# First norm of a three-block network: its weights come in as one row and are spread over the partitions by two products

## The reference, cut to what matters

```python
def _rmsnorm(x, g):
    xf = x.astype(jnp.float32)
    r = lax.rsqrt(jnp.mean(xf * xf, axis=-1, keepdims=True) + EPS)
    return (xf * r * g.astype(jnp.float32)).astype(x.dtype)
...
f = _swiglu(_rmsnorm(x, ffn1_pre_g[l]), ffn1_w_gate[l], ffn1_w_up[l], ffn1_w_down[l])
x = x + 0.5 * _rmsnorm(f, ffn1_post_g[l])
```

## Time and profile before

| | before |
|---|---|
| median of 3 runs | 2034.22 us (2034.13 to 2034.35) |
| profiled execution, its own time | 2034.27 us |
| its span | 2032.5 us |
| TensorE busy | 2015.1 us, 99% of the span |
| VectorE, GpSimd, ScalarE busy | 61%, 50%, 47% |
| granted TensorE clock, mean | 0.999 |
| DMA, mean over the span | 94 GB/s |
| DMA, 12.7 to 22.4 us | 295 GB/s |

### The profile page before, as it was taken

How to read it: one execution, slowest core, us unless ns; L and a number is a source line. 1 busy time by engine, 2 the same in 40 slices (tenths; PEclk the granted TensorE clock), 3 DMA queues, 4 the chain that set the end, 5 groups by cost and what they waited for, 6 DMA issues and landing times.

```text
span 2032.5 us, 30529 instructions
## 1 busy us (share of the span) xinstructions
PE 2015.1 (99%) x11856; PEld 1753.2 (86%) x11856; DVE 1234.5 (61%) x2038; ACT 951.5 (47%) x1777; POOL 1020.3 (50%) x576
## 2 busy tenths in 40 slices
PE   9999999999999999999999999999999999999998
PEld 8999988877788999988888878899888888888997
DVE  7877730877848777811356673965333676568553
ACT  5445623567754545623444544443433445353442
POOL 4666654346753766744434443465534443264542
PEclk9999999999999999999999999999999999999999
DMA  6333332311033333332322222333342222223332
GB/s 189 102 105 106 104 102 94 121 43 32 32 104 104 105 105 107 105 100 94 129 81 75 74 79 78 94 99 99 114 130 84 79 75 75 83 84 94 104 114 73
DMA packets 244287, 191.65 MB, mean 94 GB/s; under 512 B 6448, under 2 KB 208816, under 8 KB 243760
## 3 DMA queue, kind: packets, MB, share of 16 engines
q1 hardware_dynamic: 244144, 189.70, 30.6%
HBM read 187.58 MB, written 2.10 MB: 93 GB/s over the span
## 4 chain that ended last, share of the span: by engine, by line
PE 91%; DVE 5%; ACT 2%; issue 1%; SPq 0%; DMA 0%; POOL 0%; DVEq 0%; ACTq 0%
PE bank L2205 19%; PE bank L2206 19%; PE bank L2207 19%; PE bank L2338 9%; PE bank L2340 9%; PE bank L2339 9%; PE bank L2199 3%; PE bank L2496 1%; PE bank L2664 1%; PE bank L2516 1%; PE bank L2523 1%; DVE xs_part L1542 1%; DVE xs_lo L1567 1%; DVE xn L1441 0%; DVE x_tok L1446 0%
## 5 line engine op out<-in xcount | busy, mean ns | idle before, releaser
L708 POOL TENSOR_TENSOR w_lo<-w_raw,w_hi 128x1024 fp32r<-128x1024 f32 x216 | 536.8, 2495 | 470.2 <-ACT w_hi L864 469.8
L864 ACT ACTIVATE w_hi<-w_raw 128x1024 fp32r<-128x1024 f32 x271 | 283.2, 1053 | 197.2 <-DMA w_raw<-in_ffn_w_down 125.3
L2205 PE MATMUL bank<-xt_hi,w_hi 128*128 128x512 f32 (+1 forms) x640 | 243.4, 380 | 0.5
L2206 PE MATMUL bank<-xt_lo,w_hi 128*128 128x512 f32 (+1 forms) x640 | 239.3, 374 | 0.0
L2207 PE MATMUL bank<-xt_hi,w_lo 128*128 128x512 f32 (+1 forms) x640 | 239.3, 374 | 0.0
L2205 PE MATMUL bank<-w_hi,xt_hi 128*128 128x512 f32 (+1 forms) x456 | 178.2, 391 | 0.0
L2207 PE MATMUL bank<-w_hi,xt_lo 128*128 128x512 f32 (+1 forms) x456 | 174.4, 382 | 0.0
L2206 PE MATMUL bank<-w_lo,xt_hi 128*128 128x512 f32 (+1 forms) x456 | 174.3, 382 | 0.0
L2205 PEld LDWEIGHTS bank<-xt_hi,w_hi 128*128 128x128 f32 x640 | 120.5, 188 | 29.5 <-issue 6.7
L2207 PEld LDWEIGHTS bank<-xt_hi,w_lo 128*128 128x128 f32 x640 | 120.5, 188 | 22.0
L2206 PEld LDWEIGHTS bank<-xt_lo,w_hi 128*128 128x128 f32 x640 | 120.7, 189 | 19.6
(11 more groups left out here) (397 smaller groups left out, 5583.2 us busy)
## 6 DMA issues: line engine op xcount, KB each, us to landing
w_raw<-in_w_in SPq DMA_DIRECT2D x132, 512.0 KB, 3.8
w_raw<-in_ffn_w_down SPq DMA_DIRECT2D x44, 512.0 KB, 3.4
w_raw<-in_ffn_w_gate SPq DMA_DIRECT2D x43, 512.0 KB, 3.9
w_raw<-in_ffn_w_up SPq DMA_DIRECT2D x43, 512.0 KB, 3.8
w_raw<-in_w_out SPq DMA_DIRECT2D x24, 512.0 KB, 3.4
w_raw<-in_w_branch SPq DMA_DIRECT2D x24, 512.0 KB, 3.4
w_raw<-in_w_qkv SPq DMA_DIRECT2D x16, 512.0 KB, 3.8
x_tok<-in_x SPq DMA_DIRECT2D x4, 512.0 KB, 7.0
```

The lines of the kernel that those rows point to most:

```text
L708: pool.tensor_tensor(lo_slots[i], raw_slots[i], f32(hi_slots[i]), ALU.subtract).then_inc(lo_ready, 1)
L864: act.activation(hi_slots[i], raw_slots[i], ACT.Copy).then_inc(hi_ready, 1)
L2205: pe.matmul(out_ap, ah, bh, start=first, stop=False)
L2206: pe.matmul(out_ap, ah, bl, start=False, stop=False)
```

## The change

The row of weights is loaded as it is, 4 KB into partition 0 (`gain_row`), ahead of x chunk 0. GpSimd writes ones into a row of 128 (`one_row`). TensorE makes two products of that row of ones with the two halves of the weights' row, both operands fp32 and one partition deep, into banks 3 and 7, so that each partition there holds the weights. VectorE scales chunk 0 in two halves straight from these banks, then copies them into `g_pre`, which the later chunks read. The first half of chunk 0 now counts on `xn_first`, as that of chunk 1 did. The 36 fillers become 20 ahead of the two products and 10 behind them, and fillers write bank 6 instead of bank 7.

```diff
--- before.py
+++ after.py
@@ -183,6 +183,7 @@
             return t
 
         xn, junk = on("xn", [2, D], 88), on("junk", [D], 96, BF16)
+        gain_row, one_row = on("gain_row", [D], 98), on("one_row", [P], 0)
 
 
         def x_sum_tiles(name, home):
@@ -299,6 +300,8 @@
 
         bank = [ctx.enter_context(nc.psum_tensor(f"bank{i}", [P, SEQ], F32)) for i in range(8)]
 
+        gain_banks = (bank[3], bank[7])
+
         def f32(t):
 
             return t.bitcast(F32)
@@ -351,6 +354,7 @@
         w_used = sem("w_used")
         x_in = [sem(f"x_in{c}") for c in range(NC)]
         pre_in, post_in = sem("pre_in"), sem("post_in")
+        gain_spread = sem("gain_spread")
         tabs1_in, tabs2_in = sem("tabs1_in"), sem("tabs2_in")
         swap_in, swap_ready, count_in = sem("swap_in"), sem("swap_ready"), sem("count_in")
         decay_in = sem("decay_in")
@@ -584,8 +588,8 @@
             def load_x(c):
                 sp.dma_start(x_tok[:, c, :], x_v[:, c, :]).then_inc(x_in[c], 16)
 
+            sp.dma_start(gain_row[0:1, :], ffn1_pre_g).then_inc(pre_in, 16)
             load_x(0)
-            gain(g_pre, ffn1_pre_g, pre_in)
             load_x(1)
 
             def first_between(i):
@@ -695,8 +699,9 @@
 
         @block.gpsimd
         def _(pool):
+            pool.memset(one_row[0:1, :], 1.0).then_inc(pool_step, 1)
             pool.memset(ident[:, :], 0.0).then_inc(pool_step, 1)
-            pool.wait_ge(pool_step, 1)
+            pool.wait_ge(pool_step, 2)
             pool.affine_select(out=ident[:, :], in_=ident[:, :], compare_op=ALU.not_equal, fill=1.0, base=0,
                                pattern=[[-1, P]], channel_multiplier=1).then_inc(ident_ready, 1)
 
@@ -716,7 +721,7 @@
                 ins.then_inc(pool_step, 1)
                 pool.wait_ge(pool_step, steps[0])
 
-            steps[0] = 1
+            steps[0] = 2
 
             def out_low(pair):
 
@@ -1461,12 +1466,21 @@
 
                 dve.wait_ge(rtx_done, 4 * b + c + 1)
                 link(dve.reciprocal(inv_x[c % 2], root_x[c % 2]))
-                if c == 0:
+                if c == 0 and b > 0:
                     dve.wait_ge(pre_in, 16 * (b + 1))
                 if b in (0, 4) and c >= 2:
                     dve.wait_ge(tr_done, 2 * (4 * b + c - 1))
                 if b == 5 and c >= 2:
                     dve.wait_ge(out_done, 32)
+                if (b, c) == (0, 0):
+                    dve.wait_ge(gain_spread, 1)
+                    for half, done in enumerate((xn_first, xn_ready)):
+                        sl = cols(half, 512)
+                        dve.scalar_tensor_tensor(out=xn[:, 0, sl], in0=x_tok[:, 0, sl], scalar=inv_x[0],
+                                                 in1=gain_banks[half][:, :], op0=ALU.mult, op1=ALU.mult).then_inc(done, 1)
+                    dve.tensor_copy(g_pre[:, 0:512], gain_banks[0][:, :])
+                    link(dve.tensor_copy(g_pre[:, 512:D], gain_banks[1][:, :]))
+                    return
                 if b == 0 and c == 1:
                     dve.scalar_tensor_tensor(out=xn[:, 1, 0:512], in0=x_tok[:, 1, 0:512], scalar=inv_x[1],
                                              in1=g_pre[:, 0:512], op0=ALU.mult, op1=ALU.mult).then_inc(xn_first, 1)
@@ -2273,8 +2287,8 @@
             def turn_chunk(b, c):
 
                 for half, bk in enumerate((bank[c], bank[4 + c])):
-                    if half == 0 and (b, c) == (0, 1):
-                        pe.wait_ge(xn_first, 1)
+                    if half == 0 and b == 0 and c < 2:
+                        pe.wait_ge(xn_first, c + 1)
                     else:
                         pe.wait_ge(xn_ready, 4 * b + c + 1)
                     transposes(bk, [xn[:, c % 2, cols(4 * half + k)] for k in range(4)]).then_inc(tr_done, 1)
@@ -2421,10 +2435,15 @@
             def keep_busy(n):
 
                 for _ in range(n):
-                    pe.matmul(bank[7][:, 0:P], ident[:, :], ident[:, :], is_transpose=True)
+                    pe.matmul(bank[6][:, 0:P], ident[:, :], ident[:, :], is_transpose=True)
 
             pe.wait_ge(ident_ready, 1)
-            keep_busy(36)
+            keep_busy(20)
+            pe.wait_ge(pre_in, 16)
+            for half in range(2):
+                ins = pe.matmul(gain_banks[half][:, :], one_row[0:1, :], gain_row[0:1, cols(half, 512)], start=True, stop=True)
+            ins.then_inc(gain_spread, 1)
+            keep_busy(10)
             turn_chunk(0, 0)
             keep_busy(6)
             turn_chunk(0, 1)
```

## The result

| | before | changed |
|---|---|---|
| median of 22 runs | 2034.22 us | 2036.46 us |
| lowest, highest | 2034.05, 2034.56 | 2035.54, 2038.56 |
| profiled execution, its span | 2034.27, 2032.5 | 2038.41, 2036.6 |
| ratio to before, 95% interval | | 1.0013 (1.0007 to 1.0019) |

A forecast was written before the change was run, and what follows sets the result against it. TensorE, busy 2015.1 of 2032.5 us, was taken as the bound, so only its gapless start could move. VectorE's delay of +1.00 less 0.15 at chunk 3 gave +0.85, forecast 2035.1 us, range 2033.7 to 2036.9.

The forecast's parts named there:

- Points 1 and 2: Loads: row in front delays x chunk 0 by 0.44 us; 512 KB less brings chunk 1 1.1 to 1.9 earlier.
- point 6: VectorE: halves and two copies end at 10.52, so chunk 1 and the first feed-forward product come 1.00 us later.
- Point 3: GpSimd's memset of one row ahead of ident: 0.05 us, so fillers start at 1.58.
- Point 4, the price: The two fp32 products take four passes, 1.82 us at 2.4 GHz, plus 0.17 until the result: banks ready at 7.89.
- Point 4, the clock: Clock rise seen near 5.85 us, products starting at 5.90, so they were priced at 2.4 GHz, 1.82 us.
- second rival: The two products run at 1.2 GHz and cost 3.63 us: +2.66, 2036.9 us; chance 0.20.
- third rival: Clock stays low into the first feed-forward products: loss above 4.1 us, up to 8.5, 2042.8 us; chance 0.03.
- Point 5: Ten fillers behind the products: chunk 0's transposes start at 8.8 against 7.99, hidden because chunk 1 comes later.
- Point 7: Taken back at x chunk 3: TensorE's 0.15 us wait for its transposes goes, leaving TensorE 0.85 later.
- a sign of being wrong: Stated refutation: first feed-forward product before 12.65 us, or TensorE's gaps behind it growing.

The follow-up runs named there:

- e3: Changed kernel with 5 fillers ahead of the two products instead of 20: median 2034.96 us.
- e11: Changed kernel with 16 fillers ahead of the products instead of 20: 7 executions at 2035.08 to 2035.65 us, 4 at 2037.29 to 2037.65.
- e12: Changed kernel, GpSimd's first low part made to wait for VectorE's second half of x chunk 1: median 2035.80 us.
- e4: Changed kernel, chunk 1 also scaled from the banks, copies moved behind second slab's low part: 7 executions at 2035.22 to 2035.87 us, 4 at 2039.27 to 2039.60.
- e5: Kernel before, its 36 fillers replaced by 14 fp32 products of the identity, one partition deep: median 2034.83 us.
- e6: Kernel before, its 36 fillers replaced by 14 fp32 products of the identity, 128 partitions deep: median 2034.12 us.
- e2: Changed kernel with all 36 fillers ahead of the products, none behind: median 2039.16 us.
- e9: Changed kernel run again, nothing altered: 9 executions at 2035.76 to 2036.34 us, 2 at 2038.15 and 2038.40; gave its second trace, 2035.84.
- e1: Changed kernel with products 128 partitions deep, the row loaded behind x chunk 0: median 2035.84 us, traced execution 2034.84.
- e8: Kernel before with the first norm's weights left out, x in their place, and a 64-byte load into g_pre: median 2033.40 us.
- e10: Changed kernel, row loaded first into 32 partitions, products 128 deep, 12 fillers ahead and 8 behind, ScalarE copying: median 2033.97 us against 2034.28 before.

## Why the prediction was right or wrong

The forecast was 2035.1 in a range of 2033.7 to 2036.9; the median is 2036.46. The range holds it and the sign is right, but no execution of the changed kernel was as low as 2035.1, and the forecast's 0.85 is less than half of the 2.2 us. That the median lies inside is in part luck: 8 of 22 executions lie above the range, and the others owe some 0.7 us to a collision that no rival named.

*Points 1 and 2, the loads:* right, but for what they set free (point 6). x chunk 0 landed 0.3 to 0.5 later (4.62 and 4.75), chunk 1 at 7.06 in one trace and before 6.09 in the other (forecast 6.3 to 7.1), and VectorE had no use for it.

*Point 3:* the fillers started at 1.66, not 1.58: the extra memset costs 0.13.

*Point 4, the price:* right where the clock is up. Four records in 1.98 us against 1.82 and 0.17. The low level was priced at 3.63, with the 0.17 at 3.80, and measured 3.77 from first start to end. The Trainium skill, "FP8 and Floating Point Precision", section "TensorE Precision Notes", has four passes for true FP32; the traces agree: each product is two records, and records in mid-stream start 0.853 us apart at the low level, which is twice 512 columns at 1.2 GHz, and 0.43 at the high one.

*Point 4, the clock:* **this failed for a third of the executions.** The step took the rise at 5.85 as given, "since the clock rose right where they start". It varies from 4.8 to 6.2 over the traces, and the products, one partition deep, do not bring it: where it had not come when they began, it came 4.1 to 4.5 us after they had ended (e3, e11, e12, e4, the changed kernel), at 14.4 in the changed kernel's trace. The second rival had this, at 2036.9, but priced only the products. The trace adds ten fillers at 0.22 and eight transposes at the low level, which is the third rival's path short of its end: 2038.4, between the two. The argument against the second rival, that their operands feed the array as long as fillers do, is what e5 and e6 refute.

*Point 5:* "hidden" was right at the high level, wrong at the low one, where fillers and transposes set the start.

*Point 6:* VectorE's stretch from banks to chunk 1 was forecast as 2.84 us and is 2.83 in the second trace. The copies cost 0.60 apart and 0.68, as taken. **The sentence behind it failed:** ScalarE and GpSimd "have their order fixed by the same transposes and move no further than this". In the earlier trace rows it wasn't the transposes that held ScalarE's high part until 9.44, but the norm of chunk 1, which lands earlier now. So GpSimd starts 0.07 earlier and VectorE's half 0.76 later, and they meet. This adds 1.0 to that half and about 0.7 to the time of the first group. The prediction asked how far each engine moves, not how far apart they come to lie. Its own rows had the sign of such a collision: `xn` of chunk 3 takes 2.06 where chunk 0's, the same instruction, takes 1.28, with a low part on GpSimd from 19.03 to 21.43 beside it. The Trainium skill, "SBUF — State Buffer", section "Who interferes with whom", says that a VectorE instruction with two SBUF inputs contends with a GpSimd instruction that reads SBUF, and that the order of issue decides who waits. The traces agree: 0.75 became 1.75, 1.29 became 1.84, each for the one that came second. With VectorE's low parts beside it, which have one input in a bank, GpSimd takes 1.29 in the kernel before, and 1.28 with nothing beside it in the late trace.

*Point 7:* right at chunk 3, but the credit doesn't last. 1.55 at the first product had become 1.23 at chunk 3 and 1.17 just behind it, so 0.3 to 0.4 was taken back there, not 0.15. But near 1704 us TensorE loses 0.4 again, and the total is 1.57:

```profile
1704.70 0.47 PE L2219 MATMUL bank<-pt_hi,vr_hi 128*128 128x512 f32 x1 [0.21 <-DVE pt_lo L2075]
```

In the kernel before, the same product starts at 1703.11 without that wait. So one gap of TensorE behind the start did grow, which the prediction had named as a sign of being wrong. The wait is in the trace of every kernel here that loads the row first on SP's queue (the changed one, e2, e3, e4, e9 to e12) and in none of the others (before, e1, e5 to e8); its cause is open.

So of the 2.2 us: 0.6 is the forecast's own sum, as e1's trace has it, without that collision and with a rise ahead of the products; 0.7 is the collision (e12); 0.3 is what the late third does to the median, from 2036.18 of the first group's 14 to 2036.46 of all 22. The 0.6 that is left lies inside the first group, which is 1 us wide, and is argued, not shown. Two things that the traces hold would make it up: chunk 3 and the loss near 1704 us together, 0.2 more here than in e1; and the start of the products, which was 5.73 in e1 and is 6.12 where no filler ran at the high level, up to 0.4 later.

## What to carry to other kernels

Price a saved transfer by leaving its data out first: here the prize was 0.7 us with the loads in their old order, and the work put in its place cost more. Where TensorE runs fillers to bring its clock up, give anything that is put among them full depth, and read the level from the distance of starts, not from a mean. When a change delays one of two chains and frees the other, look for the pairs of VectorE and GpSimd instructions that used to miss each other, and read for each engine what really released it before.

## What the runs showed that was not expected

- With products one partition deep in TensorE's stream, the clock rose 9 us (e3) and 12 to 13 us (the changed kernel's late executions) after the stream's start, where streams of full depth had it up after 3.3 to 4.9 (e8, e6). They did not lower it once it was up (2 us of them, in the traces of e2 and e9).
- The moment of the rise behind the same fillers was 4.8 us in one trace and 6.2 in another.
- A 4 KB load on a second queue, issued at 1.96 us, landed 5.4 us later; 128 KB issued first on SP's queue (e10) landed after 2.4.
- The clock of the first 15 us alone split the executions in two groups 1.7 us apart. A single profile shows one of them, and the page's granted clock neither.
